# Routed expert stage: expert 0's rows picked from contiguous columns, and the prompt's output product taken chunk by chunk

## The reference, cut to what matters

```python
def trunk(x, cond, P, caches):
    for layer in range(DEPTH):                      # DEPTH = 2
        ...
        x = x + g1 * out                            # out = mixed @ w_out, 1024 x 1024
        xm = rms_norm(x, P['norm2_w'][layer]) * (1 + sc2) + sh2
        x = x + g2 * ec_moe(xm, P['router_w'][layer], P['exp_w_gate'][layer], P['exp_w_up'][layer], P['exp_w_down'][layer])

def ec_moe(x, router_w, w_gate, w_up, w_down):      # 16 experts, every one takes its top `cap` tokens
    cap = n_tok * EC_CAPACITY // N_EXPERTS          # 64 of 512 sample tokens, 16 of 128 prompt tokens
    aff = jax.nn.softmax(jnp.einsum('btd,de->bte', x, router_w), axis=-1)
    gate, idx = lax.top_k(jnp.swapaxes(aff, 1, 2), cap)
    xe = x[bidx, idx]
    hid = jax.nn.silu(jnp.einsum('becd,edf->becf', xe, w_gate)) * jnp.einsum('becd,edf->becf', xe, w_up)
    ye = jnp.einsum('becf,efd->becd', hid, w_down) * gate[..., None]
    return jnp.zeros_like(x).at[bidx, idx].add(ye)
```

## Time and the profile before

| | us |
|---|---|
| median of three runs | 1416.8 |
| the profiled execution, its own time | 1415.48 |
| its span from first to last instruction | 1413.6 |
| TensorE busy | 1324.3 (94% of the span) |
| mean granted clock of TensorE | 0.982 |

### The profile page before, as it was taken

How to read it: one execution, slowest core, us unless ns; L and a number is a source line. 1 busy time by engine, 2 the same in 40 slices (tenths; PEclk the granted TensorE clock), 3 DMA queues, 4 the chain that set the end, 5 groups by cost and what they waited for, 6 DMA issues and landing times. The chain is left out here.

```text
span 1413.6 us, 27174 instructions
## 1 busy us (share of the span) xinstructions
PE 1324.3 (94%) x11105; PEld 806.2 (57%) x11105; DVE 698.1 (49%) x1636; ACT 529.4 (37%) x1221; POOL 276.8 (20%) x237
## 2 busy tenths in 40 slices
PE   5999998889899999999989999989899999999995
PEld 1756566766686444444438998555588444444443
DVE  1536514677635333344357628866735344333435
ACT  2723113676333322222225468665523322222213
POOL 0001104596002011111100040555301011111101
PEclk7999999999999999999999999999999999999997
DMA  9688860131437999999982022050053999999985
GB/s 364 232 327 333 331 217 25 37 144 46 182 119 258 369 374 374 375 374 376 388 294 77 4 69 60 1 223 1 14 225 112 373 378 376 374 375 379 374 312 179
DMA packets 105799, 333.80 MB, mean 236 GB/s; under 512 B 23182, under 2 KB 29164, under 8 KB 99532
## 3 DMA queue, kind: packets, MB, share of 16 engines
q1 hardware_dynamic: 99276, 310.11, 57.9%
q0 software_dynamic: 5824, 19.86, 6.0%
q10 hardware_dynamic: 576, 2.10, 0.4%
HBM read 308.13 MB, written 23.89 MB: 235 GB/s over the span
## 5 line engine op out<-in xcount | busy, mean ns | idle before, releaser
L1957 PE MATMUL psum<-wraw,proj 128*32 128x512 f32 x3072 | 403.0, 598 | 7.7 <-issue 6.0
L1963 PE MATMUL psum<-wraw,proj 128*16 128x256 f32 x3072 | 235.6, 381 | 0.6 <-ACT proj L2071 0.6
L1963 PEld LDWEIGHTS psum<-wraw,proj 128*16 128x16 f32 x3072 | 90.2, 97 | 232.2 <-issue 227.4
L1957 PEld LDWEIGHTS psum<-wraw,proj 128*32 128x32 f32 x3072 | 96.8, 110 | 79.7 <-issue 15.8
L1925 POOL DMA_INDIRECT x_rows<-modrow,idx x30 | 42.9, 1429 | 452.6 <-DVE modrow L2166 452.6
L2084 ACT ACTIVATE proj<-psum 128x320 f32<-128x320 f32 x32 | 14.0, 437 | 286.5 <-PE psum L2023 286.5
L2128 DVE TENSOR_SCALAR proj<-psum,proj 128x64 f32<-128x64 f32 x232 | 55.6, 312 | 107.0 <-PE psum L1945 107.0
L1336 POOL TENSOR_SCALAR ring<-ring,small 128x640 f32<-128x640 f32 x48 | 90.3, 1886 | 39.8 <-DVE small L1275 39.4
L2161 DVE SCALAR_TENSOR_TENSOR modrow<-psum,proj 64x512 f32<-64x512 f32 x60 | 45.0, 749 | 84.2 <-PE psum L1963 83.8
L2153 DVE TENSOR_TENSOR proj<-proj,psum 64x512 f32<-64x512 f32 x32 | 22.1, 690 | 127.5 <-ACT proj L2091 127.5
L1266 DVE TENSOR_REDUCE small<-psum 128x1 f32<-128x640 f32 (+1 forms) x80 | 57.3, 717 | 52.3 <-PE psum L1241 51.8
(11 more groups left out here) (519 smaller groups left out, 2410.6 us busy)
## 6 DMA issues: line engine op xcount, KB each, us to landing
wraw<-in_exp_w_gate_dram SPq DMA_DIRECT2D x128, 512.0 KB, 16.4
wraw<-in_exp_w_up_dram SPq DMA_DIRECT2D x128, 512.0 KB, 16.8
wraw<-in_exp_w_down_dram SPq DMA_DIRECT2D x128, 512.0 KB, 16.5
ring<-in_ada_w_dram SPq DMA_DIRECT2D x29, 1024.0 KB, 6.9
hold<-in_ada_w_dram SPq DMA_DIRECT2D x14, 1024.0 KB, 6.8
ring<-in_ev_w_in_dram SPq DMA_DIRECT2D x4, 2048.0 KB, 12.3
xr<-x_rows SPq DMA_DIRECT2D x15, 512.0 KB, 7.5
proj<-in_ada_w_dram SPq DMA_DIRECT2D x5, 1024.0 KB, 9.1
```

Source lines behind the costliest of these rows:

```text
L1957: mm = pe.matmul(psum[quad(q, 32), b, :], xs[:, quad(q % 2, 32)], pair[q // 2], start=first, stop=last)
L1963: mm = pe.matmul(psum[quad(q, CAPP), b, 0:QP], xs[:, CAPS:CAP], pair[q // 2][:, q % 2 * QP:(q % 2 + 1) * QP], start=first, stop=last)
```

## The change

It has three parts, in both layers.

1. **The last tile's product** (`last_product`) takes both column halves of a chunk before the next chunk, chunks in the order 4, 5, 6, 7, 0, 1, 2, 3. After each chunk TensorE raises `chunk`, and SyncE then asks for one quarter of two matrices whose slots that chunk's weights have left (`free_chunk`): quarters of 3 and 4 after the first four chunks, of 5 and 6 after the last four. The slots of 4, 5 and 6 are permuted for it. ScalarE's copies of both halves now wait for the last chunk.
2. **The selection** of expert 0 reads `xr` in contiguous halves of 512 columns. The two column groups of the array take two tiles each, so that the two halves of the partitions hold partial sums; it starts when all four `pick` are there.
3. **`tensor_rows`** replaces the four transposes: eight fp32 matmuls, each with 128 columns of the picked rows (stride 8) as stationary operand and `both_halves` (128x64, two identity blocks on top of each other, one new VectorE addition at the stage's start) as moving operand, add the partial sums and turn them. The order of chunks in `first_hidden`, the banks, and the copy of the selection (two of 512 columns, the first when the first half is done) follow from it. One load of the next layer's weights waits for matrix 47 to be used in place of 46.

```diff
-        SLOT_AT = [("ring", 4 * 4096), ("ring", 5 * 4096), ("proj", PROJ_SLOT), ("ring", 3 * 4096), ("ring", 2 * 4096), ("ring", 0), ("ring", 4096),
+        SLOT_AT = [("ring", 4 * 4096), ("ring", 5 * 4096), ("proj", PROJ_SLOT), ("ring", 3 * 4096), ("ring", 4096), ("ring", 2 * 4096), ("ring", 0),
...
-        def load_weights(sp, l, m, ready):
+        def load_part(sp, l, m, ready, i):
 
             n, e = EXPERT_ORDER[m]
             src = A[EXPERT_W[n]][l, e].rearrange("(p k) n -> p (k n)", p=P)
-            parts = PARTS
-            w = 4096 // parts
-            for i in range(parts):
-                sp.dma_start(wraw[m % NSLOT][:, i * w:(i + 1) * w], src[:, i * w:(i + 1) * w]).then_inc(ready[m % NSLOT], 16)
+            w = 4096 // PARTS
+            sp.dma_start(wraw[m % NSLOT][:, i * w:(i + 1) * w], src[:, i * w:(i + 1) * w]).then_inc(ready[m % NSLOT], 16)
+
+        def load_weights(sp, l, m, ready):
+            for i in range(PARTS):
+                load_part(sp, l, m, ready, i)
...
-                for t in range(ST):
-                    pe.wait_ge(s["pick"], t + 1)
-                    for c in range(2):
-                        mm = pe.matmul(psum[64 * c:64 * c + CAPS, 1, :], pick[:, t, :], columns(t, 4 * c, 4 * c + 4), start=(t == 0), stop=(t == ST - 1))
-                    if t == ST - 2:
-                        turn_affinities(pe, 1)
-                mm.then_inc(selected, 1)
-                keep_busy(pe, 5, 5)
+                pe.wait_ge(s["pick"], ST)
+                for h in range(2):
+                    for j in range(2):
+                        for c in range(2):
+                            t = 2 * c + j
+                            mm = pe.matmul(psum[64 * c:64 * c + CAPS, h, :], pick[:, t, :], xr[:, t, h * 512:(h + 1) * 512], start=(j == 0), stop=(j == 1))
+                        if h == 1 and j == 0:
+                            turn_affinities(pe, 1)
+                    mm.then_inc(selected, 1)
+                keep_busy(pe, 5, 4)
+
+            def tensor_rows(pe, rows):
+
+                for k in range(KD):
+                    at = k // 2 * CAPS
+                    mm = pe.matmul(bank(5 + k % 2)[:, at:at + CAPS], rows[:, k::KD], both_halves, start=True, stop=True)
+                return mm
...
+            LAST_ORDER = (4, 5, 6, 7, 0, 1, 2, 3)
+
+            def free_chunk(sp, i):
+
+                sp.wait_ge(s["chunk"], i + 1)
+                for m in (3, 4) if i < 4 else (5, 6):
+                    load_part(sp, l, m, ready, i % 4)
...
+                        if t == ST - 1:
+                            for i in range(2):
+                                free_chunk(sp, i)
                         sp.wait_ge(s["xm"], t + 1)
                         sp.dma_start(xm_rows[t * P:(t + 1) * P, :], xm[:, t % 2, :]).then_inc(s[f"row{t % 2}"], 16)
-                    sp.wait_ge(s["mm"], 2 * TILES)
-                    load_weights(sp, l, 3, ready)
-                    load_weights(sp, l, 4, ready)
-                    load_weights(sp, l, 5, ready)
+                    for i in range(2, KD):
+                        free_chunk(sp, i)
...
+                    def last_product(lo, hi):
+
+                        for n in range(lo, hi):
+                            at, h = divmod(n, 2)
+                            k = LAST_ORDER[at]
+                            if at == 0:
+                                pe.wait_ge(s["gx"], 2 * PT + h - 3)
+                                pe.wait_ge(s["xlow"], TILES)
+                            cut = slice(h * 512, (h + 1) * 512)
+                            b = bank((2 * PT + h) % 4)
+                            pe.matmul(b, xh[:, PT % 2, k, :], wv_high[:, k, cut], start=(at == 0), stop=False)
+                            pe.matmul(b, xh[:, PT % 2, k, :], wv_low[:, k, cut], start=False, stop=False)
+                            mm = pe.matmul(b, xT_r[:, k * NT + PT * P:k * NT + (PT + 1) * P], wv_high[:, k, cut], start=False, stop=(at == KD - 1))
+                            if h:
+                                mm.then_inc(s["chunk"], 1)
...
-                    product(PT, 0, 0, 1)
+                    last_product(0, 1)
                     turn(ST - 1)
-                    product(PT, 0, 1, 3)
+                    last_product(1, 3)
                     logits(pe, ST - 1)
-                    product(PT, 0, 3, 7)
+                    last_product(3, 7)
                     turn_affinities(pe, 0)
-                    product(PT, 0, 7, KD)
-                    product(PT, 1)
+                    last_product(7, 2 * KD)
                     keep_busy(pe, 20, 3)
                     turn(PT)
...
+                            own(dve.tensor_tensor(both_halves, ident[:, 0:CAPS], ident[:, CAPS:2 * CAPS], ALU.add))
...
-                        act.wait_ge(s["mm"], 2 * PT + 1 + h)
+                        act.wait_ge(s["chunk"], KD)
                         act.activation(g2[:, h, :], bank((2 * PT + h) % 4), ACT.Copy).then_inc(s["pt"], 1)
...
-                    pe.wait_ge(s["selc"], 1)
-                    for k in range(4):
-                        mm = pe.transpose(bank(k // 2)[:, k % 2 * P:(k % 2 + 1) * P], picked_s[:, k, :], ident[:, :])
-                    mm.then_inc(s["xT"], 2)
+                    pe.wait_ge(s["selc"], 2)
+                    routed["tensor_rows"](pe, picked_s).then_inc(s["xT"], 2)
                     for m in (0, 1):
                         pe.wait_ge(ready[m], landed(m))
                     pairs = [[wraw[m][:, k * 512:(k + 1) * 512] for m in (0, 1)] for k in range(KD)]
-                    for n, k in enumerate((0, 4, 1, 5, 2, 6, 3, 7)):
+                    for n, k in enumerate((0, 2, 4, 6, 1, 3, 5, 7)):
...
-                act.wait_ge(s["sel"], 1)
-                act.activation(picked_s, bank(1).rearrange("p (k d) -> p k d", k=4), ACT.Copy).then_inc(s["selc"], 1)
+                for h in range(2):
+                    act.wait_ge(s["sel"], h + 1)
+                    act.activation(picked_s[:, h * 512:(h + 1) * 512], bank(h), ACT.Copy).then_inc(s["selc"], 1)
                 act.wait_ge(s["xT"], 2)
-                for k in (0, 4, 1):
+                for k in (0, 2, 4):
...
-                for i, used in enumerate((41, 43, 46)):
+                for i, used in enumerate((41, 43, 47)):
```

More of the change, by code:

```diff
@@ L1422, in out_and_route @@
                                               "lg", "mx", "ex", "pt", "pown", "recip", "aff", "affT", "top", "it", "st", "row0", "row1", "stp", "rowp",
-                                              "whigh", "wlow", "xhigh", "xlow", "mrow", "rwm", "shifted", "picked", "chosen", "pick")}
+                                              "whigh", "wlow", "xhigh", "xlow", "mrow", "rwm", "shifted", "picked", "chosen", "pick", "chunk")}
             HALF, B0 = NS // 2, 32
@@ L1446, in out_and_route @@
             token_of, slot_of = small[:, 48:48 + TILES], small[0:CAPS, 56:57]
+            both_halves = small[:, 64:64 + CAPS]
             ssq, rstd, mxs, sums = small[:, 0:5], small[:, 8:13], small[:, 16:21], small[:, 24:29]
@@ L1557, in tensor_prompts @@
                 for q in range(4):
-                    mm = pe.matmul(psum[32 * q:32 * q + 2 * CAPP, 3, 0:256], pick_p, columns(PT, 2 * q, 2 * q + 2), start=True, stop=True)
+                    mm = pe.matmul(psum[32 * q:32 * q + 2 * CAPP, 1, 0:256], pick_p, columns(PT, 2 * q, 2 * q + 2), start=True, stop=True)
                 mm.then_inc(selected, 1)
@@ L1563, in tensor_chosen @@
                 for e in range(2):
-                    at = CAPS + CAPP * e
-                    pe.matmul(spread[:, at:at + CAPP], ident[0:NE, e:e + 1].to_broadcast([NE, P]), idxf[0:NE, CAPS:CAP], start=True, stop=True)
+                    pe.matmul(spread_p[:, e * CAPP:(e + 1) * CAPP], ident[0:NE, e:e + 1].to_broadcast([NE, P]), idxf[0:NE, CAPS:CAP], start=True, stop=True)
                 pe.transpose(bank(7)[0:CAP, 0:NE], idxf[0:NE, :], ident[0:NE, 0:NE])
@@ L1829, in turn_copy @@
                             act.wait_ge(s["turned"], 2 * t + h + 1)
-                            if h == 0:
+                            if h == 0 and t < PT:
                                 act.wait_ge(s["mm"], 2 * t + 2)
@@ L2183, in vector @@
                 dve.wait_ge(s["xT"], 2)
-                for k in (2, 6, 3):
+                for k in (1, 3, 5):
                     modulate_picked(k)
```

35 lines of the change are left out of this document (18 added, 17 removed).

## The result

The changed kernel took 1433.65 us, the median of four runs (1424.38 to 1435.35), beside 1416.41 for the kernel before in the same comparison: a ratio of 1.010 (95% interval 1.0076 to 1.0127). Six more runs later gave 1.0066 (1.0052 to 1.0079), with a median of 1425.82. So it is slower by 0.7 to 1.0%. These fall in two groups: four took 1432.0 to 1435.7 us, with a mean granted clock of 0.965 to 0.968, and six took 1424.4 to 1427.2, at 0.973 to 0.976.

A forecast was written before the change was run, and what follows sets the result against it. Layer 0's experts were taken to go at TensorE's pace, with TensorE's road from product to first expert also counting. +2.0 us a layer, +3.9 in two, less 0.7, gave +3.2 on 1415.48: 1418.7 us, range 1413.3 to 1421.0.

The forecast's parts named there:

- Prompt product: Prompt's transposes, each layer: GpSimd's four operations in a row make them and everything behind 1.9 us later.
- Start of the selection: Selection, each layer: it waits for the fourth pick instead of the first, so starts 0.8 us later.
- Selection: Selection matmuls, each layer: contiguous reads make eight pairs at 0.43 to 0.46 us instead of 0.92, -3.9 us.
- Rows: Picked rows, each layer: eight fp32 matmuls with strided loads replace four transposes, +3.2 us.
- the two bounds: Row loads: 0.11 us apiece as when contiguous (+1.3 us a layer), or 0.235 us strided (+3.3).
- Stream: Expert weights, layer 0: the earlier stream removes one wait for a weight transfer, -0.7 us, once.
- the long beat: Layer 0's experts: one interval between hidden-row transposes of 17.88 us against 17.15, with a 0.73 us weight wait.
- The sum at full clock: Both layers: 1.9 + 0.8 - 3.9 + 3.2 makes +2.0 us a layer, +3.9 in two.
- slower, by the clock: Rival, 0.10: TensorE idle before the prompt's transposes lowers the clock for dense work behind, +2.5 us a layer, 1423.7.
- The median's excess: Whole kernel: plain runs' median 1.3 us above the profiled run, taken as weight waits that the earlier stream removes.

The follow-up runs named there:

- contig_rows: Changed kernel with ScalarE's copy writing the selection chunk by chunk, so the eight row matmuls load contiguous columns; 1419.92 us, ratio 1.0018.
- requests_only: Kernel before with only the early weight requests, chunk by chunk in half 1, half 0 still finished first; 1415.90 us, ratio 1.0002.
- late_turn: Kernel before with 29 filler matmuls in place of 20 ahead of the prompt's transposes; 1423.96 us, ratio 1.0064.
- late_dense: Kernel before with 8 fillers of 512 columns in place of the 20 of 128 ahead of the prompt's transposes; 1424.19 us, ratio 1.0065.
- fill_turn: Changed kernel with 29 filler matmuls in place of 20, meant to fill TensorE's idle wait for GpSimd; 1426.60 us, ratio 1.0059.
- before_again: Kernel before, run once more unchanged as a control; 1417.95 us, ratio 1.0012.
- sel_only: Kernel before with only the new contiguous selection and eight row matmuls; product, slots and requests as before; 1424.46 us, ratio 1.0052.
- prod_only: Kernel before with only the chunk-wise product and its early requests; selection and transposes as before; 1424.13 us, ratio 1.0045.
- wide_rows: Changed kernel with 128 columns streamed in place of 64 in each row matmul, at the same strided loads; 1426.35 us, ratio 1.0045.
- after_dense: Changed kernel with 8 fillers of 512 columns in place of the 20 of 128; 1430.32 us, ratio 1.0105.
- combo_dense: Changed kernel with half 0 finished first, contiguous row loads, selection from the second pick, 5 fillers of 512 columns for the 20; 1413.41 us, ratio 0.9992.

## Why the prediction was wrong, point by point

- *Prompt product, +1.9:* right. GpSimd's four operations stand in a row, and the transposes are 2.02 us later. This is POOL's timeline after, beside the earlier trace rows:

```profile
436.47 1.27 POOL L1857 TENSOR_TENSOR proj<-proj,hold 128x512 f32<-128x512 f32 x1 [84.63 <-ACT proj L1892]
437.82 1.27 POOL L1858 TENSOR_TENSOR xr<-xr,proj 128x512 f32<-128x512 f32 x1
439.26 1.26 POOL L1857 TENSOR_TENSOR proj<-proj,hold 128x512 f32<-128x512 f32 x1 [0.18 <-POOL xr L1858]
440.60 1.26 POOL L1858 TENSOR_TENSOR xr<-xr,proj 128x512 f32<-128x512 f32 x1
```

- *Start of the selection, +0.8:* right, 0.75.
- *Selection, -3.9:* right at full clock. From its start to the rows 452.11 - 446.95 = 5.16 us in contig_rows, 9.03 before, so -3.87. In the changed kernel it is 6.60 in layer 0, since 1.44 go to the clock.
- *Rows, +3.2:* right, 3.36. The choice between the two bounds held: 0.235 us apiece strided. That a matmul's load reads its operand twice, from which I had worked it out, no run shows: a strided load lasts 143 ns more than a contiguous one where the working had 124. The Trainium skill's section "LDWEIGHTS (loading the stationary operand)" in "TensorE: Matmul & The Clock Gate" is contradicted by the trace as a rule for every layout: 335 ns strided and 192 contiguous for the same 128 columns.
- *Stream, -0.7:* right in size. requests_only shows that the early requests are enough to remove the long beat, with no shift in the stage. But the beat is gone in late_turn and late_dense as well, which ask no earlier and only run their experts 2 us later: a kernel made that late would have lost the wait anyway.
- *The sum at full clock:* +2.26 a layer against +2.0. It was never the problem.
- **The step that failed** is the rival "slower, by the clock", with the assumption in all other cases that the granted clock stays at 1.00 in the stage. The measured clock is 0.58 and 0.50 there. I gave the rival 0.10 and hung it on the idle stretch of 1.85 us, because the only fall that I had read, came behind an idle stretch. fill_turn shows that the idle stretch is not needed. I priced it at 2.5 us a layer; the falls cost 5.7 and 5.1 in the profiled execution. The greater part hangs on the step that I had summed with care for its duration alone: the rows. I had asked how long sixteen loads take, and not what the clock does behind 4 us in which TensorE is paced by loads and streams 64 columns at a time. That the direction came out as in this rival is no credit to it: its condition was the wrong one.
- *The median's excess:* I took it as waits for weights. before_again points to the clock in its place (1414.07 us at a mean clock of 0.982, 1426.57 at 0.973). No run shows the waits for which I took the 1.3 us, so that step was not supported either.

What stays open: why the falls at the selection's start come in one layer and not in the other of the same kernel; what the new product adds to the rows' fall, which sel_only has in one layer and for 3.4 us only; which of the falls the shorter executions of the changed kernel lack; and why late_turn, late_dense, prod_only and sel_only, with 4.6, 4.8, 5.2 and 3.4 us of shift in the stage, are 7 to 9 us slower in the median. Their profiles put 3 to 6 us of it outside the stage, where those of before differ by 11 among themselves.

## What to carry to other kernels

Where a change puts load-paced matmuls of few columns on the path, look at the granted clock of what follows, not only at their own duration: here 4 us of rows were followed by 4 us more in the first expert. Let the copy that must be made anyway do the rearranging, so that the loads become contiguous. And before one execution is taken as the base of a sum, look at how the mean clock and the time of the other runs scatter: 13 us here, far more than the terms that were summed.

## What the runs showed of the hardware

- A load of 128 fp32 columns at a stride of 8 words lasts 335 ns and comes every 0.235 us, a contiguous one 192 ns and every 0.11 us. ScalarE's rearranging copy takes 0.60 us, as the plain one does, and the rows start 2.23 us behind the selection's last records in both.
- The granted clock fell to 0.50 with TensorE busy throughout ahead of the fall (3.00 of 3.00 us): for 10 us behind sixteen 64-column records at 0.235 us (window 458 to 468), and not behind the same records with 128 columns (wide_rows, 1.00 in both layers). In sel_only it did not fall in layer 0.
- With eight fillers of 512 columns in place of those of 128 the clock stayed at 1.00 at the selection's start in 4 of 4 stages that were about 2 us late (late_dense, after_dense), and with five of them in 1 of 2 (combo_dense); late_dense gained nothing in the total over late_turn.
- The same program ran its attention of layer 1 at 0.52 in one execution and at 1.00 in another.
